# Two-branch attention of a small hybrid transformer: from one head a step to two heads a step, with half-array score matmuls

## The reference

```python
def attend(q, k, v, scale):
    s = jnp.einsum('bhqd,bhkd->bhqk', q, k).astype(jnp.float32) * scale
    p = jax.nn.softmax(s, axis=-1).astype(v.dtype)
    return jnp.einsum('bhqk,bhkd->bhqd', p, v)

# mla_branch: multi-head latent attention, head size 96 (64 + 32 rotary), values 64 wide
    k_all = jnp.concatenate([kc, kl], axis=2)
    o = attend_blocked(ql, k_all, v_all, scale)
# natten_branch: neighbourhood attention, head size 64; a bias and a column mask on the latent keys
        s_win = jnp.einsum('bhqd,bhrkd->bhqrk', q_row, k_band).astype(f32) * scale + bias
        s_win = jnp.where(col_ok[:, None, :], s_win, NEG_INF)
        s_ctx = jnp.einsum('bhqd,bhcd->bhqc', q_row, kc).astype(f32) * scale
        p = jax.nn.softmax(jnp.concatenate([s_win.reshape(b, h, GRID_W, n_band), s_ctx], axis=-1), axis=-1)
```

## Time and profile before

| | |
|---|---|
| median of 3 runs | 1773.76 us (1771.92 to 1777.18) |
| the profiled execution: time, span | 1772.61 us, 1770.9 us |
| PE busy | 1637.0 us, 92% of the span |
| DVE, ACT, POOL busy | 992.3, 759.2, 670.4 us |
| mean granted TensorE clock | 0.972 of full |
| chain that ended last: PE | 74% |

### The profile page before, as it was taken

The page is one execution under the profiler, slowest core; times in us unless marked ns, Lnnn a source line. Parts: engine busy times, 40 slices in busy tenths (PEclk is TensorE's granted clock), DMA queues, the critical chain, the costliest instruction groups (busy, mean ns, idle before and its releaser), DMA issues.

```text
span 1770.9 us, 24625 instructions
## 1 busy us (share of the span) xinstructions
PE 1637.0 (92%) x9536; PEld 1383.1 (78%) x9536; DVE 992.3 (56%) x1739; ACT 759.2 (43%) x1470; POOL 670.4 (38%) x389
## 2 busy tenths in 40 slices
PE   7998989899999989899999998978899988889998
PEld 3876769766877668688888886967897876789998
DVE  5855825855275545359596964134136385546655
ACT  4333654344544443442323234247444644454443
POOL 0532334611343002355454553534551551133442
PEclk9999999999999999999999999989999999989999
DMA  8532525410225022134354743122521242235553
GB/s 336 198 141 78 201 92 166 176 39 1 98 96 183 26 102 92 51 143 143 142 191 166 285 167 119 66 95 79 155 96 48 93 140 96 99 133 193 178 188 119
DMA packets 69851, 230.63 MB, mean 130 GB/s; under 512 B 18280, under 2 KB 24808, under 8 KB 56424
## 3 DMA queue, kind: packets, MB, share of 16 engines
q1 hardware_dynamic: 60880, 213.67, 34.4%
q10 hardware_dynamic: 8856, 15.39, 2.4%
HBM read 216.45 MB, written 12.58 MB: 129 GB/s over the span
## 4 chain that ended last, share of the span: by engine, by line
PE 74%; DVE 10%; ACT 7%; issue 3%; POOL 3%; DMA 1%; ACTq 0%; POOLq 0%; DVEq 0%; SPq 0%
PE bank L1747 37%; PE bank L1829 9%; PE bank L1785 8%; PE bank L1767 4%; PE bank L2114 4%; PE bank L2093 3%; PE bank L1811 2%; PE bank L2100 2%; ACT wH L776 2%; POOL wL L663 1%; DVE mjunk L1204 1%; PE bank L1978 1%; DVE arena L1275 1%; POOL wL L665 1%; DVE acc L1207 1%
## 5 line engine op out<-in xcount | busy, mean ns | idle before, releaser
L663 POOL TENSOR_TENSOR wL<-raw,wH 128x1280 fp32r<-128x1280 f32 (+3 forms) x146 | 302.7, 2073 | 556.4 <-ACT wH L776 556.4
L665 POOL TENSOR_TENSOR wL<-raw,wH 128x768 fp32r<-128x768 f32 (+3 forms) x198 | 329.1, 1662 | 368.2 <-ACT wH L776 368.2
L776 ACT ACTIVATE wH<-raw 128x768 fp32r<-128x768 f32 (+6 forms) x396 | 296.7, 806 | 395.6 <-PE bank L1747 295.5
L1747 PE MATMUL bank<-hH,wH 128*128 128x512 f32 (+1 forms) x720 | 248.8, 346 | 5.2 <-DVE wL L1189 3.2
L1747 PE MATMUL bank<-hH,wL 128*128 128x512 f32 (+1 forms) x720 | 245.5, 341 | 0.0
L1747 PE MATMUL bank<-hL,wH 128*128 128x512 f32 (+1 forms) x720 | 245.4, 341 | 0.0
L1747 PE MATMUL bank<-oH,wH 128*128 128x512 f32 (+1 forms) x576 | 196.6, 341 | 2.9 <-DVE oL L1611 2.9
L1747 PE MATMUL bank<-oL,wH 128*128 128x512 f32 (+1 forms) x576 | 195.3, 339 | 0.0
L1747 PE MATMUL bank<-oH,wL 128*128 128x512 f32 (+1 forms) x576 | 195.2, 339 | 0.0
L1207 DVE SCALAR_TENSOR_TENSOR acc<-acc,cb 128x1024 f32<-128x1024 f32 x88 | 168.7, 1930 | 2.5
L1747 PEld LDWEIGHTS bank<-hH,wH 128*128 128x128 f32 x720 | 137.3, 191 | 22.8 <-DVE wL L1189 3.8
(11 more groups left out here) (216 smaller groups left out, 3234.0 us busy)
## 6 DMA issues: line engine op xcount, KB each, us to landing
raw<-in_p_ff SPq DMA_DIRECT2D x64, 1024.0 KB, 4.8
acc<-in_p_mod SPq DMA_DIRECT2D x44, 1024.0 KB, 5.7
raw<-in_p_ml SPq DMA_DIRECT2D x12, 1024.0 KB, 5.1
raw<-in_p_na SPq DMA_DIRECT2D x12, 1024.0 KB, 5.7
raw<-in_p_mgc SPq DMA_DIRECT2D x16, 512.0 KB, 3.6
raw<-in_p_mga SPq DMA_DIRECT2D x16, 512.0 KB, 3.5
raw<-in_p_mgb SPq DMA_DIRECT2D x16, 512.0 KB, 3.8
raw<-in_p_out SPq DMA_DIRECT2D x8, 1024.0 KB, 4.8
```

Of the source, the lines that this page charges most:

```text
L663: pool.tensor_tensor(l_[:, 0:cut], r_[:, 0:cut], h_[:, 0:cut].bitcast(F32), ALU.subtract)
L665: pool.tensor_tensor(l_[:, cut:k * w], r_[:, cut:k * w], h_[:, cut:k * w].bitcast(F32), ALU.subtract)\
L776: act.activation(flat(wH, n)[:, part], flat(raw, n)[:, part], ACT.Copy)\
L1747: ins = pe.matmul(dst, w_[:, kk, c:c + P], r_[:, kk, lo:TOK], start=kk == k0 and m == 0, stop=kk == k0 + kn - 1 and m == 2)
```

## The change

Each step of the loop takes two heads. `head_pairs` lists 16 turns in layer 0 and 8 in layer 1. The probabilities have four buffers in each branch (`s_probs`), and so have the maxima and sums in `stat`. The output matmuls come one step after the scores, not two, and the side work lies between the transposes and the output matmuls, 6 or 12 matmuls at a time. On DVE, outputs and side results of earlier turns come ahead of this turn's maxima.

The na scores use `a_q` with two heads stacked in the 128 partitions and no zeros. Heads 2g and 2g+1 lie in partitions 0 to 63 and 64 to 127 of queries and keys, so each matmul has 64 rows of the array; and instead of one matmul of 512 (or 256) columns a head there are pieces of 128 columns, which alternate between the two halves. The bias now has 256 zeros somewhere ahead of it, and one addition of 512 columns from PSUM, with zeros on the context half, replaces copy and addition. The scores of the next turn wait only for `max` there, since ACT reads the exponential's input from SBUF.

Besides, block na 0 becomes `SHARED`, with a `share_ahead` on DVE just ahead of the barrier after ml; the memset on POOL shrinks from 4096 to 256 columns; and ACT writes na queries in pieces of 128 partitions, half as many.

```diff
+def head_pairs(l):
+    return [(qi, t, g) for qi, t in enumerate(att_tiles(l)) for g in range(HEADS // 2)]
...
-        a_q, a_k, a_v, a_tb = view(0, 8, TOK), view(4096, 4, TOK), view(6144, 4, 512), view(8192, 8, 6, 64)
+        a_q, a_k, a_v, a_tb = view(0, 4, TOK), view(2048, 4, TOK), view(4096, 4, 512), view(8192, 8, 6, 64)
+        A_ZERO, A_TB = 7936, 8192
...
-        SHARED = [name in ("to", "wo") or (name == "ml" and j < 2) or (name, l) == ("ff", 1) for name, l, j in KEYS]
+        SHARED = [name in ("to", "wo") or (name == "ml" and j < 2) or (name, j) == ("na", 0) or (name, l) == ("ff", 1) for name, l, j in KEYS]
...
-            return -(-KC * 12 // (len(att_tiles(l)) * HEADS))
+            return -(-KC * 12 // len(head_pairs(l)))
...
-                pool.memset(a_q, 0.0).then_inc(S(f"na{l}_zero").handle, 1)
+                pool.memset(view(A_ZERO, CTX), 0.0).then_inc(S(f"na{l}_zero").handle, 1)
...
@@ ACT
+                    for s in range(len(turns) + 2):
...
+                        if 1 <= s <= len(turns):
+                            nk = att_keys(turns[s - 1][1]) * P
+                            for i in range(2):
+                                k = 2 * s - 2 + i
+                                act.wait_ge(*S(tag + "pt").at(k + 1))
+                                if k >= 2:
+                                    act.wait_ge(*S(tag + "o").at(k - 1))
+                                act.activation(s_pt[:, i, 0:nk], bank[6 + i][:, 0:nk], ACT.Copy).then_inc(S(tag + "pts").up(1), 1)
+                        if s < len(turns):
+                            qi, t, g = turns[s]
+                            nk = att_keys(t) * P
+                            for i in range(2):
+                                k = 2 * s + i
+                                probs = s_probs[br][k % 4][:, 0:nk]
+                                act.wait_ge(*S(tag + "max").at(k + 1))
+                                if k >= 4:
+                                    act.wait_ge(*S(tag + "pt").at(k - 3))
+                                    act.wait_ge(*S(tag + "oev").at(k - 3))
+                                act.activation(probs, probs if br == "na" and t >= 2 else bank[4 + i][:, 0:nk], ACT.Exp,
...
@@ DVE
+                share_ahead(N["gate", l, gate_range(l, "last").stop - 1])
                 end()
...
+                    for s in range(len(turns) + 2):
+                        if s >= 2:
+                            qi, t, g = turns[s - 2]
+                            for i in range(2):
+                                k, h = 2 * s - 4 + i, 2 * g + i
+                                dve.wait_ge(*S(tag + "o").at(k + 1))
+                                link(dve.reciprocal(stat[:, 24 + i:25 + i], stat[:, 20 + k % 4:21 + k % 4]))
...
                         for c in range(KC):
-                            if side_step(l, c) + 1 == step:
+                            if side_step(l, c) + 1 == s:
                                 branch_out(br, l, c)
-                            if br == "mla" and side_step(l, c) + 3 == step:
+                            if br == "mla" and side_step(l, c) + 2 == s:
                                 share_ahead(N["ms", l, c])
+                        for i in range(2 if s < len(turns) else 0):
+                            qi, t, g = turns[s]
+                            k, h, nk = 2 * s + i, 2 * g + i, att_keys(t) * P
+                            src = bank[4 + i][:, 0:nk]
+                            dve.wait_ge(*S(tag + "s").at(k + 1))
...
+                                bias = view(A_ZERO, 2, step)[:, :, 0:CTX]
+                                scores = s_probs[br][k % 4]
+                                link(dve.tensor_tensor(scores.rearrange("p (a w) -> p a w", a=2),
+                                                       src.rearrange("p (a w) -> p a w", a=2), bias, ALU.add))
...
+                            dve.reduce_max(stat[:, 16 + k % 4:17 + k % 4], src, axis=AX,
+                                           negate=True).then_inc(S(tag + "max").up(1), 1)
+                            if i == 0:
+                                attended(s)
...
@@ PE
+                    for s in range(len(turns) + 2):
+                        if s < len(turns):
+                            qi, t, g = turns[s]
+                            if s:
+                                moved = br == "na" and turns[s - 1][1] >= 2
+                                pe.wait_ge(*S(tag + ("max" if moved else "p")).at(2 * s))
                             if br == "na":
-                                q_, k_ = a_q[:, h, t * P:t * P + P], a_k[:, h // 2, 0:nk]
+                                for c in range(att_keys(t)):
+                                    for i in range(2):
+                                        r = slice(64 * i, 64 * i + 64)
+                                        ins = pe.matmul(bank[4 + i][:, c * P:c * P + P], a_q[r, g, t * P:t * P + P],
+                                                        a_k[r, g, c * P:c * P + P], start=True, stop=True)
...
+                        if 1 <= s <= len(turns):
+                            for i in range(2):
+                                k = 2 * s - 2 + i
+                                pe.wait_ge(*S(tag + "p").at(k + 1))
...
+                                    ins = pe.transpose(bank[6 + i][:, c * P:c * P + P], s_probs[br][k % 4][:, c * P:c * P + P], ident)
+                                ins.then_inc(S(tag + "pt").up(1), 1)
+                        if br == "na" and s == 1:
+                            drained(u0 + 6)
+                            pump(extra, 2 * pace)
+                        elif s < len(turns) and (br == "mla" or s):
+                            pump(extra, pace)
+                        if 1 <= s <= len(turns):
+                            qi, t, g = turns[s - 1]
...
+                                pe.wait_ge(*S(tag + "pts").at(k + 1))
+                                if k >= 2:
+                                    pe.wait_ge(*S(tag + "oev").at(k - 1))
+                                if i and g == 0 and qi > 0:
+                                    pe.wait_ge(*S(tag + "oL").at(qi))
```

More of the change, by code:

```diff
@@ L409, in build @@
         st, s_sq, s_sq2 = view(11264, 2, 512), view(12288, 512), view(15360, 512)
-        s_p, s_pt, s_o = view(12800, 2, 512), view(13824, 2, 512), view(14848, 2, 512)
+        s_pt, s_o = view(13824, 2, 512), view(14848, 2, 512)
+        s_probs = dict(na=[view(at, 512) for at in (6144, 6656, 7168, 12800)],
+                       mla=[view(at, 512) for at in (12800, 13312, 10240, 10752)])
         l_t = view(10624, NTILE, ROPE)
@@ L988, in queries_out @@
                         if br == "na":
[L989 to L995, removed]
+                            for tt in range(ntl):
+                                src = tb[:, tt * 256:tt * 256 + 256].rearrange("p (a t) -> p a t", a=2)
+                                dst = a_q[:, h0 // 2:h0 // 2 + 2, (t + tt) * P:(t + tt) * P + P]
+                                ins = act.activation(dst, src, ACT.Copy, scale=gcols[:, 0:1])
                             ins.then_inc(S(tag + "trq").up(1), 1)
@@ L1065, in _ @@
                             ahead(N["na", l, j])
[L1067 to L1076, removed]
[L1077 to L1092 removed]
+                    turns = head_pairs(l)
+                    for s in range(len(turns) + 2):
+                        if s >= 2 and turns[s - 2][2] == HEADS // 2 - 1:
+                            qi, t, _ = turns[s - 2]
                             act.wait_ge(*S(tag + "ot").at(qi + 1))
@@ L1570, in _ @@
                         dve.wait_ge(*S(tag + "rpb").at(12 * 16))
+                        dve.wait_ge(*S(tag + "zero").at(1))
                         mask = const[:, C_MASK:C_MASK + GRID_W].rearrange("p (a w) -> p a w", a=1)
@@ L1608, in _, with attended @@
+                    turns = head_pairs(l)
+                    def attended(s):
+                        if s >= 2 and turns[s - 2][2] == HEADS // 2 - 1:
+                            qi, t, _ = turns[s - 2]
                             dve.wait_ge(*S(tag + "oH").at(qi + 1))
@@ L1619, in _ @@
+                        if s >= len(turns):
+                            attended(s)
                     if br == "mla":
```

129 lines of the change are left out of this document (39 added, 90 removed).

## The result

The changed kernel takes 1730.1 us (median of 4 runs, 1726.73 to 1732.9) against 1773.99 (4 runs, 1771.92 to 1777.18) for the kernel before on the same chip: a ratio of 0.975, 95% interval 0.9727 to 0.9773. Measured again, beside 7 runs of before, it came out as 0.974 (0.9723 to 0.9757). So the change takes 44 us off. The prediction, 1747 with a range of 1736 to 1761, gave 27 and is wrong in its size.

What follows compares the result with a forecast made beforehand. PE, 92% busy, was taken as the bound on latent tiles, with some waiting on context tiles. Gains 4.3 + 17.7 + 5.2 = 27.2 from 1772.6 gave 1745.4; with 1.2 added, taken as 1747 us, range 1736 to 1761.

Steps and rivals of the forecast that it cites:

- the loops at the old price of the scores: Four attention loops, score matmuls costed as before: PE's work taken as the length, plus ends and waits; gain 17.7 us.
- 1.8 for the clock in the first loop: Na loop, layer 0: 1.8 us added for a mean clock of 0.98 over 92.2 us.
- The na scores: Na score matmuls on PE: halves stream side by side, loading costs 0.07 us a pass; 10.5 less 5.3, net gain 5.2.
- The switch: PE changing between 128 and 64 rows, twice a turn, 44 times on the path: 0.12 us each, 5.3 in all.
- Block na 0: Start of na's projections in both layers: DVE takes POOL's first part, PE starts 2.15 us earlier; gain 4.3 us.
- No overlap: Rival for the na scores: weight loads queue, so the halves don't help; 1761 us with full switches, chance 0.22.
- the slower case: Rival for the na scores: alternating halves makes each pass pay its whole length; about 1796 us, chance 0.05.
- Full overlap: Rival for the na scores: two halves run at once, switching is free; 14.4 instead of 5.2, 1737 us, chance 0.25.
- The pair loop's waits: Rival in the attention loops: next scores come late behind DVE's outputs and side results; 12 us, so 1758, chance 0.08.
- What was to be seen: Signs: PE's first na matmul 2.1 us earlier, wait near 3.5; turns 3.7, 5.8, 6.1; no idling at new tiles' outputs.

Runs made afterwards that it cites:

- `scores_full_512`: Changed kernel with each head's na scores as one matmul over all 128 rows and up to 512 columns (wrong scores, timing only): 1738.14 us, ratio 0.9782.
- `scores_half_512`: Changed kernel with each head's na scores as one 64-row matmul of 512 (256) columns instead of alternating 128-column pieces: 1731.11 us, ratio 0.9745.
- `before_block_shared`: Kernel before with only block na 0 given to DVE and POOL (the SHARED edit and the share_ahead call): 1771.39 us, ratio 0.9967.
- `block_not_shared`: Changed kernel with block na 0 done by POOL alone, as before: 1733.84 us (1727.59 to 1736.67).

## Why the prediction was right in direction and wrong in size

- **The step that failed:** "On a latent tile the four pieces of PE work follow each other without a gap ... There PE itself is the bound, and only a shorter matmul helps." A step of the kernel before was a ring through PE, DVE, ACT and back, closed by two slots for maxima and sums. With four slots and no other edit the time falls by 22 us (1777.14 to 1754.86), and PE's same matmuls take 0.84 and 0.44 for 0.93 and 0.55. The prediction saw the wait for `oev` on context tiles alone, and then multiplied the stretched pieces into its sum for the new loop.
- **The term that this made too small:** the loops at the old price of the scores, 17.7. By the loop sum of `scores_full_512` it is 305.4 - 271.9 = 33.5, of which the slots bring 21.5 and the rest of the change in the loops, pairs above all, 12.0. The stretched pieces explain nearly all of the gap. Transposes and outputs of a latent head were put at 0.55 + 0.93 and take 0.435 + 0.865, so 0.18 too much for each of 64 latent heads, 11.5. With 0.11 for each of 32 context heads, 3.5, that is 15.0, against 33.5 - 17.7 = 15.8. One term erred the other way: 1.8 for the clock in the first loop, where the window after, 76.2 us at 0.95, makes it 3.8.
- **The na scores,** net 5.2 forecast: the medians of `scores_full_512` and the changed kernel differ by 7.9, the loop sums by 8.2. A latent pair was put at 1.12 and takes 1.09, and a context pair with its switch at 0.80 and takes 0.65 + 0.15. The reason chosen had two parts. That the halves run side by side holds. That a load of 0.07 us sets the pace doesn't: `scores_half_512` has a quarter of the loads and takes the same time. So 0.07 a pass came out right by luck. The switch was put at 0.24 a turn, and 0.15 shows in the transposes. The Trainium skill's page "TensorEngine Tiling (Array Packing)", Key Properties, has a change of mode drain TensorE: the traces agree that a change costs something, 0.15 us a turn, and don't show what it is. By the Trainium skill's page "TensorE: Matmul & The Clock Gate", Part 3, The mechanism, row groups run concurrently: the traces agree, with 1.06 us for two 512-column matmuls in two halves against 1.77 over all rows, 0.18 more than the half of it.
- **Block na 0,** 4.3 forecast: the waits shrink by 2.9. POOL's second part was put at its 1.81 alone, and takes 2.48 beside DVE. So the mechanism holds, and by the waits the term was 1.4 too large. By time alone 4.3 lies inside what was measured (3.5 to 8.2 from the interval), which the clock blurs.
- **The rivals.** No overlap (1761) and the slower case fell: the score passes follow each other at 1.09 / 16 = 0.068 us. Two readings behind the first were off: with the prediction's own 1.79 for 1.72 a pair, scores without overlap cost 1.2 more and not 1.9, and the 0.116 a pass, its argument for a limit in the load, was stretched by the ring (1.73 / 16 = 0.108). Full overlap (1737) had its mechanism nearly right, 1.06 to 1.09 a pair where it had 0.90, with a price of switching against it; by time alone it came nearest of all, and it missed because it has the same stretched loops in its sum. The pair loop's waits did not come: PE's timeline has two waits of 0.4 us or more in the first loop, 7.36 ahead of its second turn's scores and 0.57 at its last output transposes.
- **What was to be seen.** PE's first matmul of na comes 2.42 us earlier (2.1 forecast), 1.44 of it by the wait, which is 4.27 (3.5 forecast), and the rest because ml ended 0.98 earlier in this trace. The turns are 3.46, 5.24 and 5.77 for forecasts of 3.7, 5.8 and 6.1: all three too high, for the most part by the stretched pieces. PE no longer idles at the outputs of a new tile, as forecast.

## What to carry to other kernels

A chain that shows one engine without a gap is no proof that the engine is the bound. Look at each other engine's idle row: if one waits in every step for something that comes from the engine at hand (here ACT's exponential, 28.9 us, all of it for one line), follow the ring round and add it up. The idle row alone proves nothing: with four slots ACT's exponential still waits in most steps, 22.8 us from 384 to 430 us, but for its own maximum, and the step is the plain sum of PE's pieces. If the sum closes in the length of the step, the step may be the ring, and a further slot of whatever small thing is waited for is a cheap way to try it. Here four more columns in a table of row statistics were worth 22 of the 44 us, two more large buffers nothing, and turns of two heads without those columns took some 58 us more than with them.

A second reading to carry over: take the duration of a piece from a place where nothing that it waits for is late, or it brings the old wait into the sum for the new kernel.

## What the runs showed of the hardware beyond that

- Two float32 matmuls of 64 rows in the two halves of the array overlap for most of their length: 1.06 us for a pair of 512 columns that takes 1.77 over 128 rows. Alternating short pieces isn't needed for it. Eight passes of 128 columns in one half and then eight in the other hardly overlap, 1.64; four and then four do as well as alternating ones, 0.65 for both.
- A weight load that waits for a late operand lengthened a PE piece by about 0.1 us here although the chain shows no gap: 0.55 and 0.44 for four transposes, 0.93 and 0.84 for eight output matmuls, all the same instructions.
- POOL's 768 columns took 1.81 us alone and 2.48 beside a DVE operation of the same kind that ran for 1.49; the DVE operation kept its usual length, 1.492 in the earlier trace rows. It is so at both layers, and in `before_block_shared` too (2.48 four times), while the kernel before and `block_not_shared`, without the DVE operation beside it, have 1.79 to 1.81. There POOL's 768 columns follow its own 1280 and not idle time. A single row that follows idle time with DVE still, in the kernel before at 31 us, takes 1.82, so the DVE operation and not the idle time is the likely cause.
